# The first layer's mixing of a hybrid decoder step: the state scan taken tile by tile between the projections, the long convolution cut into runs, the output projection by tiles

## The reference, cut to what matters

```
def even_mixer(h, ...):
    a_val, a_gate, z, xbc, dt_raw = split_cols(h @ w_in, E_SPLIT)
    u = a_val * jax.nn.sigmoid(a_gate)
    ua, conv_a_new = causal_dw_conv(u, conv_a_prev, conv_a_w, conv_a_b)
    ya = jax.nn.silu(layer_norm(ua, ln_a_g, ln_a_b))
    xbc_c, conv_b_new = causal_dw_conv(xbc, conv_b_prev, conv_b_w, conv_b_b)
    xs, bm, cm = split_cols(jax.nn.silu(xbc_c), ...)
    dt = jax.nn.softplus(dt_raw.astype(F32) + dt_bias.astype(F32))
    a = -jnp.exp(a_log.astype(F32))
    y, ssm_new = ssd_scan(xh, dt, a, bm, cm, ssm_prev, chunk)
    y = y + d_skip.astype(F32)[:, None] * xh.astype(F32)
    y = y.reshape(b, L, D_INNER) * jax.nn.silu(z.astype(F32))
    y = y * lax.rsqrt(jnp.mean(y * y, axis=-1, keepdims=True) + EPS)   # by groups
    out = jnp.concatenate([ya, yb], axis=-1) @ w_out
```

## Time and profile before

| what | value |
|---|---|
| median of 3 runs | 2070.79 us (2067.76 to 2074.35) |
| the profiled execution | 2072.11 us, its span 2070.3 us |
| mean granted TensorE clock | 0.889 of full |
| busy in the span | PE 1741.9 us, DVE 1225.1, ACT 805.0, POOL 81.2 |
| first layer's mixing | 29.0 us (first projection matmul) to 453.7 us (last residual add) |

### The profile page before, as it was taken

How to read it: one execution, slowest core, us unless ns; L and a number is a source line. 1 busy time by engine, 2 the same in 40 slices (tenths; PEclk the granted TensorE clock), 3 DMA queues, 4 the chain that set the end, 5 groups by cost and what they waited for, 6 DMA issues and landing times.

```text
span 2070.3 us, 23126 instructions
## 1 busy us (share of the span) xinstructions
PE 1741.9 (84%) x8038; PEld 1316.0 (64%) x8038; DVE 1225.1 (59%) x1447; ACT 805.0 (39%) x871; POOL 81.2 (4%) x111
## 2 busy tenths in 40 slices
PE   6996767788999988784168976999999999999994
PEld 4753444338988845554035645878788888888883
DVE  1793232215433413399951027788888888978884
ACT  1115111003222212205022024676767676767671
POOL 3001002001000002000000001000000000000001
PEclk9997557899999999886669777999999999999997
DMA  8302003149654531202224426899999999999993
GB/s 276 121 36 88 0 11 105 38 141 387 221 165 152 167 135 29 62 16 69 70 66 117 162 82 241 312 396 334 396 333 396 347 396 334 391 350 361 369 349 95
DMA packets 237640, 420.00 MB, mean 203 GB/s; under 512 B 29030, under 2 KB 100839, under 8 KB 237434
## 3 DMA queue, kind: packets, MB, share of 16 engines
q1 hardware_dynamic: 223762, 371.98, 50.5%
q0 software_dynamic: 11504, 38.70, 5.4%
q10 hardware_dynamic: 2304, 8.39, 1.0%
HBM read 384.37 MB, written 34.98 MB: 203 GB/s over the span
## 4 chain that ended last, share of the span: by engine, by line
PE 62%; DVE 17%; SPq 8%; issue 5%; ACT 4%; DMA 2%; POOL 1%; DVEq 0%; ACTq 0%; POOLq 0%
PE psum L1123 54%; DVE zone L1946 4%; DVE zone L1945 4%; SPq L591 3%; SPq L597 3%; DVE lo L2131 3%; SPq L576 2%; PE psum L1514 1%; PE psum L1261 1%; PE psum L1259 1%; PE psum L1523 1%; DMA zone<-state_ssm 1%; PE psum L1602 1%; PE psum L1309 1%; ACT parts L1055 1%
## 5 line engine op out<-in xcount | busy, mean ns | idle before, releaser
L1123 PE MATMUL psum<-parts 128*128 128x512 f32 (+3 forms) x3692 | 929.4, 364 | 34.4 <-DVE parts L1843 17.0
L1123 PEld LDWEIGHTS psum<-parts 128*128 128x128 f32 (+1 forms) x3692 | 641.8, 188 | 144.7 <-DVE lo L2131 16.3
L2131 DVE TENSOR_TENSOR lo<-raw,parts 128x2048 fp32r<-128x2048 f32 x264 | 593.0, 2288 | 103.4 <-ACT parts L1055 103.4
L1055 ACT ACTIVATE parts<-raw 128x2048 fp32r<-128x2048 f32 x264 | 491.4, 1916 | 70.7 <-PE psum L1123 57.4
L1123 PE MATMUL psum<-lo,parts 128*128 128x512 f32 (+1 forms) x1120 | 429.2, 383 | 0.0
L1123 PE MATMUL psum<-arena 128*128 128x320 f32 (+8 forms) x1218 | 310.2, 414 | 15.6 <-ACT arena L852 7.1
L1123 PEld LDWEIGHTS psum<-arena 128*128 128x128 f32 (+2 forms) x1218 | 203.8, 202 | 125.8 <-issue 64.1
L1123 PEld LDWEIGHTS psum<-lo,parts 128*128 128x128 f32 x1120 | 212.8, 190 | 38.8
L1123 PE MATMUL psum<-arena,zone 128*128 128x512 f32 (+6 forms) x454 | 147.6, 497 | 10.1 <-DVE zone L1758 6.7
L1843 DVE TENSOR_TENSOR parts<-arena,parts 128x1024 fp32r<-128x1024 f32 x66 | 77.3, 1220 | 96.0 <-ACT parts L924 96.0
L1123 PEld LDWEIGHTS psum<-arena,zone 128*128 128x128 f32 (+4 forms) x454 | 77.0, 212 | 81.4 <-issue 65.2
(11 more groups left out here) (327 smaller groups left out, 1005.6 us busy)
## 6 DMA issues: line engine op xcount, KB each, us to landing
raw<-o_we_gate SPq DMA_DIRECT2D x40, 2048.0 KB, 10.2
raw<-o_we_up SPq DMA_DIRECT2D x40, 2048.0 KB, 11.6
raw<-o_we_down SPq DMA_DIRECT2D x40, 2048.0 KB, 10.8
arena<-e_w_in SPq DMA_DIRECT2D x7, 2048.0 KB, 18.1
slot_x<-arena POOLq DMA_DIRECT2D x1, 12288.0 KB, 38.4
arena<-e_w_gate SPq DMA_DIRECT2D x11, 1024.0 KB, 5.4
arena<-e_w_up SPq DMA_DIRECT2D x11, 1024.0 KB, 7.9
arena<-e_w_down SPq DMA_DIRECT2D x11, 1024.0 KB, 10.0
```

What stands on the lines that cost most here:

```text
L1055: act.activation(hi_ring[u % NHI][:, o:o + HALF], raw_unit(u)[:, o:o + HALF], ACT.Copy).then_inc(sem("unit_hi"), 1)
L1123: return pe.matmul(dst, w, m, start=start, stop=stop)
L2131: dve.tensor_tensor(lo_unit(u)[:, o:o + HALF], raw_unit(u)[:, o:o + HALF], hi_ring[u % NHI][:, o:o + HALF].bitcast(F32), ALU.subtract).the ...
```

## The change

The three tiles' scans are taken apart into functions (`sums`, `spread`, `within`, `states`, `turn_y` on PE; matching ones on ACT and DVE), and written in a new order between the projections. Gate and value channels 0 and 1 come first (their weights as two 1 MB pieces), xbc with dt after its fourth channel, gates 2 and 3, the transposes of x, `sums(0)`, values 2 and 3, `spread(0)`, z of tile 0, `within(0)`, `states(0)`; then tile 1 and tile 2 likewise with their own z between spread and within. The tail transposes are divided into 8 groups that stand around `spread(1)`. The layer norm's sums and the first tile's output projection stand inside the loop over batches (at batches 0, 1 and 4), where add_new(b) stands ahead of the turn of the next old state, for which there are two `h_oldT`. The output projection goes by tiles: 12 k steps of one tile and half into one bank.

On DVE the 124 tap pairs of the long convolution are cut into runs: 7 ahead of the short convolutions, 3 behind each of these, then 13, 5, 8, 8, 8, 4, 6, 8 between the scan's steps, and the last 21 ahead of the loop over batches. `d_skip` times x goes to GpSimd (`skip(i)`). Tails of the short convolution are stored earlier; output weights are asked for after the last z group. Cut to its core:

```
+        pieces0 = [(("e_w_in", 0, 8, 512, 256), ("e_w_in", 0, 8, 0, 256))] + \
+                  [(("e_w_in", 0, 8, 2048 + 512 * i, 512),) for i in range(3)] + \
...
+        used0 = {3: ("val_mm", 2), 4: ("xbc_mm", 4), 5: ("xbc_mm", 8), 6: ("xbc_mm", 12), 7: ("z_mm", 6), 8: ("val_mm", 4),
+                 9: ("z_mm", 6), 10: ("z_mm", 6)}
...
+            def skip(i):
+                n = TILES[i][2]
+                pool.wait_ge(sem("xdt_ready"), i + 1)
+                v = x_tok[0:n, i, :].rearrange("p (h q) -> p h q", h=NH)
+                pool.tensor_tensor(v, v, rows["e_d_skip"][0:n].unsqueeze(2).to_broadcast([n, NH, HP]), ALU.mult
+                                   ).then_inc(sem("skip_ready"), 1)
...
+            rsqrt(grs, gms, 2, 2)
+            pool.wait_ge(sem("p_ssm_ready"), 2)
+            load(out["p_ssm"][0, 0].rearrange("(c h) p n -> (h p) c n", h=2), h_new[0], "p_ssm_stored")
+            skip(2)
+            rsqrt(grs, gms, 2, 3)
...
+            scan_exps(2)
+            gate_z(2, 0)
+            gate_z(2, 1)
+            act.wait_ge(*reached("dA_sum_mm"))
+            act.activation(decs, bank(0)[:, 0:64].rearrange("p (c b) -> p c b", c=KD),
+                           ACT.Exp).then_inc(*reaches("decs_ready"))
+            group_squares(1)
...
+            pe.wait_ge(*count("x_tok_ready", 9))
+            spread(0)
+            pe.wait_ge(*arrival(5))
+            z_columns(0, 0)
+            pe.wait_ge(*arrival(6))
+            pe.wait_ge(sem("u_ready"), 3)
+            z_columns(0, 1)
+            pe.wait_ge(sem("u_ready"), 4)
+            within(0)
+            states(0, (3, 4))
...
+            states(1, (4, 0))
+            pe.wait_ge(*count("z_ready", 4))
+            turn_y(0)
+            pe.wait_ge(sem("p_state_ready"), 4)
...
+            for b in range(NB):
+                add_new(b)
+                if b + 1 < NB:
+                    turn_old(b + 1)
+                from_old(b)
...
+                elif b == 4:
+                    for h in range(2):
...
+                        mix_out(0, h)
+            for h in range(2):
+                pe.wait_ge(sem("x_ready"), h + 1)
+                mix_out(1, h)
+            pe.wait_ge(sem("x_ready"), 4)
+            turn_y(2)
+            pe.wait_ge(sem("mixT_ready"), 6)
             for h in range(2):
...
+                mix_out(2, h)
...
+            y_turned(0)
+            long_conv(8)
+            dve.wait_ge(sem("state_mm"), 2)
+            dve.wait_ge(*reached("inter_mm"))
+            v = p_state.rearrange("p (h q) -> p h q", h=NH)
+            own.link(dve.tensor_tensor(v, v, per_head(e_last, P), ALU.mult))
...
+            within_taken(1)
+            skip_and_gate(1)
...
+            group_mean(1)
+            weights(2)
+            group_norm(1)
+            y_turned(1)
+            within_taken(2)
+            long_conv(CA * WA - taps_done[0])
+            for b in range(NB):
+                batch_state(b)
```

More of the change, by code:

```diff
@@ L817, in _ @@
+            gate(0)
+            gate(1)
+            for c in range(4):
+                take_xbc(c)
             act.wait_ge(*reached("dt_mm"))
@@ new lines, in _ @@
+            pe.wait_ge(sem("y_taken"), 1)
+            within(1)
+            for g in range(NG):
+                ins = mm(bank(2 + g), xbcT[:, 10 + g, P:2 * P], p_state[:, 512 * g:512 * g + 512], True, True)
+            ins.then_inc(*reaches("inter_mm"))
+            states(1, (4, 0))
+            pe.wait_ge(*count("z_ready", 4))
+            turn_y(0)
+            pe.wait_ge(sem("p_state_ready"), 4)
+            pe.wait_ge(sem("mixT_ready"), 2)
+            for g in range(2):
+                for c in range(4):
+                    ins = pe.transpose(bank(1 + 4 * g, 4, P)[:, c, :], p_state[:, (4 * g + c) * P:(4 * g + c + 1) * P], ident)
+                ins.then_inc(sem("p_ssmT_mm"), 1)
@@ new lines, in _ @@
+            sums(2)
+            pe.wait_ge(sem("y_taken"), 2)
+            spread(2)
+            for h in range(2):
+                pe.wait_ge(sem("p_ssm_ready"), h + 1)
+                z_columns(2, h)
+            pe.wait_ge(*reached("dA_rows_ready"))
+            for c in range(KD):
+                ins = mm(bank(0)[:, 8 * c:8 * c + 8], dA_rows[0:NS, c * P:(c + 1) * P], K["batch"][0:NS, :], True, True)
+            ins.then_inc(*reaches("dA_sum_mm"))
+            within(2)
+            pe.wait_ge(*count("z_ready", 6))
@@ new lines, in long_conv @@
+            def long_conv(pairs):
+                for _ in range(pairs):
+                    c, j = divmod(taps_done[0], WA)
+                    taps_done[0] += 1
+                    if j == 0:
+                        dve.wait_ge(sem("u_ready"), c + 1)
+                    (dst_p, dst_s), taps = tokens(ua, c), vecA[:, c, :]
+                    for dst, src in ((dst_p, u_p[:, c, j:j + SEQ]), (dst_s, u_s[:, c, :, j:j + NT])):
+                        if j:
+                            own.wait(1)
+                            ins = dve.scalar_tensor_tensor(dst, src, taps[:, j:j + 1], dst, ALU.mult, ALU.add)
+                        else:
+                            ins = dve.tensor_scalar(dst, src, taps[:, 0:1], taps[:, 31:32], ALU.mult, ALU.add)
+                        if j == WA - 1 and dst is dst_s:
+                            ins.then_inc(sem("ua_ready"), 1)
+                        else:
+                            own.mark(ins)
@@ new lines, in within_taken, with add_old @@
+                own.wait()
+                dve.sem_inc(sem("y_taken"), 1)
+            def add_old():
+                n = NS
+                dve.wait_ge(sem("inter_acc"), 2 * NB)
+                for g in range(2):
+                    own.mark(dve.tensor_tensor(xdt[0:n, 8 * g:8 * g + 8, :], bank(2 + g, 8, HP)[0:n],
+                                               e_cum[2][0:n, 8 * g:8 * g + 8].unsqueeze(2).to_broadcast([n, 8, HP]), ALU.mult))
+                own.wait()
+                own.link(dve.tensor_tensor(y[0:n], y[0:n], xdt[0:n], ALU.add))
@@ new lines, in _ @@
+            dve.wait_ge(*reached("dt_log_ready"))
+            own.link(dve.scalar_tensor_tensor(dts, raw_dt, 0.0, dt_log, ALU.max, ALU.add))
+            dve.wait_ge(*reached("neg_a_ready"))
+            dve.tensor_tensor(dA, dts, neg_a.unsqueeze(1).to_broadcast([P, 3, NH]), ALU.mult).then_inc(*reaches("dA_ready"))
+            long_conv(13)
+            sums_taken(0)
+            times_dt(0)
+            long_conv(5)
+            gated(2)
+            gated(3)
+            times_end(0)
+            long_conv(8)
@@ new lines, in _ @@
+            weights(0)
+            long_conv(8)
+            dve.wait_ge(sem("state_mm"), 1)
+            for g in range(2):
+                dve.tensor_copy(p_state[:, 512 * g:512 * g + 512], bank(3 + g)).then_inc(sem("p_state_ready"), 1)
+            sums_taken(1)
+            times_dt(1)
+            within_taken(0)
+            skip_and_gate(0)
+            times_end(1)
+            long_conv(8)
+            group_mean(0)
+            long_conv(4)
+            weights(1)
+            dve.wait_ge(sem("kv_stored"), 32)
@@ new lines, in _ @@
+            within_taken(1)
+            skip_and_gate(1)
+            sums_taken(2)
+            times_dt(2)
+            times_end(2)
+            own.mark(dve.memset(c_pad.rearrange("p a b c -> p (a b c)"), 0.0))
+            own.wait()
+            for b in range(NB):
+                ins = dve.tensor_copy(c_pad[:, :, b, NT * b:NT * b + NT], xbcT[:, 10:12, SEQ + NT * b:SEQ + NT * b + NT])
+            ins.then_inc(*reaches("c_pad_ready"))
+            dve.tensor_copy(dA_rows[0:NS].rearrange("p (h q) -> p h q", h=NH), per_head(dA[:, 2, :], NS)).then_inc(*reaches("dA_rows_ready"))
@@ L1831, in _ @@
+            add_old()
+            skip_and_gate(2)
+            group_mean(2)
+            group_norm(2)
+            mixed(1)
+            y_turned(2)
+            mixed(2)
             norm(1, vecD[:, :, 1])
```

784 lines of the change are left out of this document (416 added, 368 removed).

## The result

The changed kernel takes 2013.5 us (median of 4 runs, 2006.4 to 2016.7), the kernel before 2072.3 in the same measurement: ratio 0.9715, 95% interval 0.9683 to 0.9747. That is 58.8 us less, where 50.4 was forecast; 2013.5 lies in the forecast's range and in that of its likeliest case (2008 to 2032). The profiled execution was the fastest of the four, 2006.4 us (span 2004.5), 65.7 us under that of before.

The account below looks back on a forecast made before the run. It took a chain through PE, ACT, DVE and POOL per tile as the bound, with PE idle 75 us in the mixing. Nine steps ended the mixing at 403.3, not 453.7: 2072.1 - 50.4 - 1.3 = 2020 us, range 1996 to 2040.

Parts of the forecast that it names:

- likeliest case: The whole kernel as the forecast's terms sum it: 2020 us, own range 2008 to 2032; chance 58%.
- nine lengths: Mixing in order: channels and dt, x turns, tile 0, tile 1, p_state, tile 2, last taps, batch loop, last output tiles.
- signs that it named as wrong: A spread at 1.00, a product near 160 us, DVE busy from 128 to 270, a batch loop over 87 us.
- Steps 5 and 7: Ahead of p_state's turn, 8.4 us, and of the first batch, 12.8 us: PE waits for DVE, taps on the path.
- Step 6: Tile 2's spread, z pair and product, with waits for DVE and ACT's late squares of tile 1: 41.5 us.
- The loop: Loop over batches, chain kept, with layer norm sums and first output tile in it: 65.8 + 20.9, so 86.7 us.
- steps 3 and 4: Tile 0's spread, z, product and states, 32.6 us; tile 1's sums, turns, spread, z and product, 46.7 us.
- The row of clock 0.50: In the kernel before, from 203.2 to 219.3, PE was busy 16.04 of 16.10 us, yet at clock 0.50.
- The rival of the full clock: Spreads and batch loop run at the full clock: 22 us more saved, 1999 us; chance 15%.
- The rival of DVE as the path: Taps and scan steps stretch beside GpSimd's products, or waits double the filler's 17.2 us on the path: 2037 us; 5%.
- The slower rival: GpSimd's d_skip product costs as much as its powers, three of 162 us: 181 us lost, 2252 us; chance 3%.

Follow-up runs that it names:

- the gap experiment: The changed kernel with PE made to wait ahead of tile 1's spread until DVE has done 8 tap pairs: 2024.5 us, 16.8 more than unaltered.

## Why the prediction was right

Its sum was made of nine lengths. Forecast and measured, in us: 85.4 and 83.5; 13.6 and 13.4; 32.6 and 27.6; 46.7 and 37.1; 8.4 and 8.1; 41.5 and 42.4; 12.8 and 13.3; 86.7 and 89.5; 46.6 and 44.5. The mixing was forecast to end at 403.3 and ended at 388.2. Two of the signs that it named as wrong did show: spreads at 1.00, and a loop of 89.5 us where 87 was the limit. That the medians lie so near (2013.5 against 2020) is in part luck: the forecast was built on the profiled execution, which came 15.3 us under it (2006.4 against 2021.7), and the other three runs of the change are 5.6 to 10.3 us slower than that one, for which the sum has no term. In the two later profiles of the same kernel the mixing took 363.0 and 362.5 us, not 359.4.

- **Right:** what PE waits for in the new order. Steps 5 and 7, with DVE's taps on the path, came within 0.5 us, and the runs that moved the taps took those waits away. Step 6, with ACT's late squares, came within 1 us, and the run that moved them shows 3.3 us of it. The loop kept its chain, 2.8 us longer than summed. The first loads of what follows did not matter: behind the last add the kernel takes 1616.3 us, before 1616.6.
- **Mis-sized:** the clock of the narrow stretches in steps 3 and 4, which hold 14.6 of the 15.1 us by which the end differs. I took 12 us for `spread(0)`, between its two ends, and 16.1, the low end, for `spread(1)`; both took 8.5 at the full clock, 11.1 less together, and the z pairs behind them started at that clock, where I had put 1.4 us each. The row of clock 0.50 was carried over to `spread(1)` as if it were a property of the spread; the gap experiment shows that it goes with the start behind idle time. For `spread(0)` a part of the difference is this execution's luck: in the twelve profiles it took 8.5 to 13.2 us. `spread(2)`, which starts behind idle time, took 8.4 us at 0.50, as summed.
- **The rival of the full clock** (1999) came true for two spreads of three and not for the loop, whose clock is 0.84 with an output tile in it. The Trainium skill ("TensorE: Matmul & The Clock Gate", Part 1) has activity release the throttle; that a spread starts at the full clock behind dense work and at the low one behind a wait agrees with it. That eight of twelve of tile 0's fell on the way, and that the one behind the gap stayed low throughout, both with PE busy without a break, is not explained by that sentence.
- **The rival of DVE as the path** had its mechanism right: taps stretched beside GpSimd's products, by 1.65 and 2.03 us. But they stood where no engine waited for them, so it cost nothing; the 17.2 us of taps on the path stayed as summed.
- **The slower rival** is out: GpSimd's products took 2.0, 1.9 and 2.9 us, far from the 162 of its powers:

```profile
119.11 2.00 POOL L727 TENSOR_TENSOR zone<-zone,arena 128x1024 f32<-128x1024 f32 x1 [95.59 <-DVE arena L1869]
...
162.06 1.92 POOL L727 TENSOR_TENSOR zone<-zone,arena 128x1024 f32<-128x1024 f32 x1
...
205.23 2.92 POOL L727 TENSOR_TENSOR zone<-zone,arena 64x1024 f32<-64x1024 f32 x1 [2.88 <-DVE arena L1869]
```

- **Partly wrong by the experiments:** that z between spread and product is the cover that makes the gain. It is worth some 7 to 12 us, and only against a version without taps on the path.

What stays open: which part of the 10 us between runs of one kernel is the clock in the mixing and which lies behind it, what makes a spread fall at one place or another, and how the gain divides between the overlapped scans, the taps and the output by tiles.

## What to carry to other kernels

The price of a narrow stretch is read together with what stands ahead of it: the same records cost 8.5 us behind dense matmuls and 16 behind a wait, so filling PE's idle time can pay twice. When a long, free job is cut into runs as filler, put the runs where the engine that does them waits, and look in the trace whether any run stands ahead of something that another engine waits for: here the last 29 of 124 pairs cost 17 us, with 23 us of idle time on the same engine just ahead of most of them. A product that is moved to GpSimd to relieve DVE is checked in DVE's rows beside it: here it cost DVE more time than it took away, where that time was free. Differences under the spread of the runs are read from the stretch that an edit touches, from a row that ends one wait to a row that ends another.

## What was not expected of the hardware

A spread that starts at the full clock loses it on the way in most executions, with PE busy throughout and with the same instructions, but at different places: tile 0's in eight of twelve, four of them early (12.8 to 13.2 us in place of 8.5). And GpSimd's products and DVE's instructions hold each other up, each in turn. Beside the products of tiles 0 and 1 DVE lost: its taps took 1.65 and 2.03 us longer, and the products 2.00 and 1.92 us. Beside that of tile 2 GpSimd lost: its product over 64 partitions took 2.92 us, in each of the twelve profiles that have it, longer than those over 128. It started with a DVE product of two operands in SBUF, which took its usual 1.22 us at 205.17:

```profile
205.17 1.22 DVE L1877 TENSOR_TENSOR arena<-arena,zone 64x1024 f32<-64x1024 f32 x1
```

The Trainium skill ("SBUF — State Buffer", Who interferes with whom) has such a pair exclude each other, with the loser blocked for the whole instruction. Taps, which also read two operands in SBUF, that are 1.65 and 2.03 us longer beside products of 2.00 and 1.92 us agree, and so does a product that is 1.0 us longer beside an unchanged instruction of 1.22 us; no run has the product of 64 partitions by itself, so its price alone is not shown.
